# A decoder step on one core: the residual loaded by quarters, operand jobs some slots on, four transpose banks at the start, and five instead of six paired output units

## The chip, the core and the metric

The kernel runs on one core of a Trainium2 chip. The metric is the time of the program in microseconds of device time. A core has a matrix engine (TensorE, PE in the rows, with its weight loads shown apart as PEld), a vector engine (DVE), a scalar engine (ACT), a general one (GpSimd, POOL) and SyncE (SP), which here issues nearly all transfers. Each engine runs its own instructions in program order and waits on semaphores. What the others do costs time only where PE comes to wait for it.

## The reference, cut to what matters

One layer: RMSNorm of the tokens (512 of a prompt, 8 of a sample), one input projection, three kinds of attention (differential, dilated window, cross-attention into 256 memory tokens), gates, one output projection with residual, and a last RMSNorm.

```python
m = rms_norm(mem, g_mem); kv = einsum('bmd,de->bme', m, w_mem_kv)   # 8 "memory" tiles
h = rms_norm(x, g_norm);  z  = einsum('bsd,de->bse', h, w_in)       # 56 "input" tiles
od, ow, om = diff_attn(...), dilated(...), memory_attn(...)
cat = concat([rms_norm(od, g_sub) * (1 - lam_init) * silu(gd), ow * silu(gw), om * silu(gm)])
y = rms_norm(x + einsum('bse,ed->bsd', cat, w_out), g_final)        # 16 "output" tiles
```

The model width is 2048, so each projection sums over 16 blocks of 128, called kt 0 to 15. All is float32. Each matrix operand is split into a high and a low part, and a product is three matmuls: high by high, high by low, low by high.

## The kernel before

**Tiles, ops and slots.** A tile is 128 output columns for all tokens (520; 256 for a memory tile). A tile multiplied singly is four ops (`quarter`, L1088), each with four of the 16 kt: 12 matmuls of 256 columns for a memory tile, 24 of 260 for an input or output tile. Of the 16 output tiles 0 and 1 are single, 2 to 13 go in six pairs, and 14 and 15 stand at the end, each in two parts. A pair (`product`, L1114) is computed by seven block products (Strassen's scheme in Winograd's form), two ops each, so 14 ops of 12 matmuls: 168 in place of 192 for two single tiles. There are 364 ops. The program of every engine is laid out by slots, one per op: in slot s PE does op s and then the jobs that `plan` put there. ACT and DVE in slot s first split the weights of op s + 3 (`split_hi` L1342, then `split_lo` L1668, which needs the high part), and then do the slot's jobs. `plan` sorts jobs of one slot by a rank, and leaves those of the same rank in the order in which it put them. The output projection begins at slot `IN_END` = 256.

**The start.** PE transposes the memory tokens (`prep`, eight jobs u = 0 to 7 of four 128x128 blocks, L1019) into the two PSUM banks of `s_ps` in turn; ACT makes the high part `act_hi` from the bank (L1331), DVE the low part `act_lo` (L1621), and only then is the bank free. PE's order is: prep 0 to 3, op 0, prep 4 and 5, op 1, prep 6 and 7, op 2. Op r of tile 0 needs u = 2r and 2r + 1. `FIRST_SPLITS` says after which u the weights of ops 0 to 4 are split. The job ("mem", "rstd") scales the memory tiles: DVE makes `r_diag` (L2058), PE multiplies it with ones (L1261), DVE copies `r_mem` from the result (L2061), and each memory tile's `evac` (L1760) needs that. `squares(i)` on ACT (L1320) sums a token block's squares, POOL makes the factor, and `scale_tokens(i)` on DVE (L1611) applies it. `natural(n)` transposes a finished tile into the one bank `t_ps` on PE (L1134), ACT copies it to `k_nat` (L1431), and SP stores it; the transposes wait until ACT has emptied `t_ps`, and the copy waits until the store before it has landed.

**The junction at `IN_END`.** Output ops need `cat` (the gated attention outputs) split: ACT makes `act_hi` (L1588) and DVE `act_lo` (L2136), for kt 0 to 3 in slot `IN_END` - 3, 4 to 7 in the next, up to 12 to 15 in `IN_END`. Op `IN_END` + r needs kt up to 4r + 3. Kt 15 comes last from the gate of tile 63 (`evac` on DVE, L1766 and L1774, in slot `IN_END`). For the pairs, `operand_add` (a "T add", four DVE instructions L1737 to L1742) makes sums of blocks of `cat`, and `operand_hi` (L1421) and `operand_lo` (L1749) split them (a "T split"); `T_ADDS`, `T_SPLITS` and `T_SPLIT_AT` give their slots. The residual `x_prompt` is loaded over `cat` into `nat`, 4 MB, by four transfers in slot `IN_END` + 3, after the last T add and the last `act_lo`; SP's later weight loads are issued behind them.

**Pairs.** In each pair DVE also adds weight tiles (`weight_sum`, L1684 to L1692) and takes the products out (`part_out`). A single output tile is copied by ACT (L1395). For each output tile `natural` transposes it, DVE adds the residual (`y_add`, L2007) and multiplies the tile before by g_final (`times_g`, L1998), and ACT sums its squares (L1576), at the slots of `Y_NAT_AT`.

## Time and profile before

| | us |
|---|---|
| three runs: median (lowest, highest) | 1031.95 (1031.47, 1033.26) |
| the profiled execution, its own time | 1031.1 |
| its span, first to last instruction | 1029.3 |
| granted TensorE clock, mean over the span | 0.996 |
| busy: PE, DVE, ACT, POOL | 1001.1, 735.3, 444.6, 54.2 |
| HBM traffic over the span | 196 GB/s |

The times of rows count from the span's start. Of the profiled execution's 1031.1 us, 1.8 lie outside the span.

### The profile page before, as it was taken

What the parts mean: (1) busy time and instruction counts of PE and PEld (TensorE: products, weight loads), DVE (VectorE), ACT (ScalarE), POOL (GpSimd) and SP (SyncE); (2) the same over time, 40 slices, a digit from 0 to 9 for tenths busy, and PEclk for the clock granted to TensorE, in tenths of its full rate; (3) what the DMA queues carried; (4) which work ended last, traced back from release to release, by engine and by line L of the source; (5) the groups of instructions that cost most, each with busy time, mean ns of one, the idle gap of its engine ahead of it and who ended that gap; (6) DMA issues with size and microseconds to landing.
All of it is one profiled execution on the core that took longest, in us unless ns stands there. A gap on an engine that the chain in (4) does not pass through costs nothing. (4 is left out here: it accounts for less than half of the span.)

```text
span 1029.3 us, 24065 instructions
## 1 busy us (share of the span) xinstructions
PE 1001.1 (97%) x8079; PEld 979.1 (95%) x8079; DVE 735.3 (71%) x2708; ACT 444.6 (43%) x1174; POOL 54.2 (5%) x122
## 2 busy tenths in 40 slices
PE   6999999999999999999999999999999999999995
PEld 6999999999999999999999999999999999999995
DVE  5783267777888777778777667577774697788874
ACT  5763222223333333444433544225665365555552
POOL 0200000000000000000000000000001000000002
PEclk9999999999999999999999999999999999999998
DMA  9863289987978877776775686997753325433224
GB/s 298 247 195 107 64 265 255 290 288 218 271 223 248 266 238 222 219 229 200 235 217 171 191 262 173 250 284 245 213 167 106 116 71 195 122 104 104 83 83 166
DMA packets 254521, 203.31 MB, mean 198 GB/s; under 512 B 12481, under 2 KB 207671, under 8 KB 253751
## 3 DMA queue, kind: packets, MB, share of 16 engines
q1 hardware_dynamic: 253934, 200.67, 65.3%
q8 instruction: 64, 1.05, 0.4%
q10 hardware_dynamic: 464, 1.12, 0.3%
q14 instruction: 59, 0.48, 0.2%
HBM read 189.98 MB, written 11.76 MB: 196 GB/s over the span
## 5 line engine op out<-in xcount | busy, mean ns | idle before, releaser
L1088 PE MATMUL z<-act_hi,w_hi 128*128 128x260 f32 (+1 forms) x1984 | 428.9, 292 | 2.5 <-DVE act_lo L2136 2.0
L1088 PE MATMUL z<-act_hi,w_lo 128*128 128x260 f32 (+1 forms) x1984 | 410.1, 283 | 0.0
L1088 PE MATMUL z<-act_lo,w_hi 128*128 128x260 f32 (+1 forms) x1984 | 409.4, 283 | 0.0
L1088 PEld LDWEIGHTS z<-act_hi,w_hi 128*128 128x128 f32 x1984 | 312.3, 189 | 7.9 <-issue 5.4
L1088 PEld LDWEIGHTS z<-act_lo,w_hi 128*128 128x128 f32 x1984 | 310.7, 189 | 0.0
L1088 PEld LDWEIGHTS z<-act_hi,w_lo 128*128 128x128 f32 x1984 | 310.3, 189 | 0.0
L1668 DVE TENSOR_TENSOR w_lo<-w_raw,w_hi 128x512 fp32r<-128x512 f32 x300 | 205.8, 688 | 120.6 <-ACT w_hi L1342 119.5
L1342 ACT ACTIVATE w_hi<-w_raw 128x512 fp32r<-128x512 f32 x300 | 185.3, 625 | 189.3 <-PE z L1088 162.1
L1857 DVE CUSTOM_DVE_ANT_0 pages<-pages,q_bc 128x128 f32<-128x128 f32 x640 | 144.3, 286 | 24.7 <-DMA pages<-in_cache_k_win_dram 12.7
L1886 DVE SCALAR_TENSOR_TENSOR v_acc<-pages,dec_a,v_acc 128x256 f32<-128x256 f32 x224 | 94.3, 477 | 2.2 <-DMA pages<-in_cache_v_diff_dram 2.1
L1464 ACT ACTIVATE probs<-probs,st_n 128x128 f32<-128x128 f32 (+3 forms) x48 | 26.8, 558 | 79.9 <-DVE st_n L1796 79.5
L1114 PE MATMUL z<-t_hi,w_hi 128*128 128x260 f32 x192 | 55.3, 288 | 1.1 <-DVE w_lo L1668 1.1
L1114 PE MATMUL z<-t_hi,w_lo 128*128 128x260 f32 x192 | 54.2, 283 | 0.0
L1114 PE MATMUL z<-t_lo,w_hi 128*128 128x260 f32 x192 | 54.2, 282 | 0.0
L1857 DVE DVE_READ_ACCUMULATOR2_ANT dec_s<- 128x1 f32 x640 | 52.3, 82 | 0.0
L1342 ACT ACTIVATE w_hi<-w_sum 128x512 fp32r<-128x512 f32 x48 | 30.2, 630 | 41.9 <-DVE w_sum L1692 15.7
L1482 ACT ACTIVATE probs_T<-t_ps 128x512 f32<-128x512 f32 (+3 forms) x40 | 18.8, 469 | 68.2 <-PE t_ps L1174 55.9
L1789 DVE CUSTOM_DVE_ANT_0 probs<-s_ps,bias 128x128 f32<-128x128 f32 (+3 forms) x48 | 22.3, 489 | 35.8 <-PE s_ps L1147 22.7
L1668 DVE TENSOR_TENSOR w_lo<-w_sum,w_hi 128x512 fp32r<-128x512 f32 x48 | 33.0, 687 | 16.8 <-ACT w_hi L1342 16.8
L1114 PE MATMUL z<-act_hi,w_hi 128*128 128x260 f32 x144 | 41.5, 288 | 2.1 <-DVE w_lo L1668 2.1
L1114 PE MATMUL z<-act_lo,w_hi 128*128 128x260 f32 x144 | 40.7, 283 | 0.0
L1114 PE MATMUL z<-act_hi,w_lo 128*128 128x260 f32 x144 | 40.7, 283 | 0.0
(232 smaller groups left out, 1161.7 us busy)
## 6 DMA issues: line engine op xcount, KB each, us to landing
w_raw<-in_w_in_dram SPq DMA_DIRECT2D x224, 256.0 KB, 4.4
pages<-in_cache_k_diff_dram SPq DMA_DIRECT2D x128, 256.0 KB, 4.9
pages<-in_cache_v_diff_dram SPq DMA_DIRECT2D x128, 256.0 KB, 3.5
w_raw<-in_w_out_dram SPq DMA_DIRECT2D x64, 256.0 KB, 2.8
w_raw<-in_w_mem_kv_dram SPq DMA_DIRECT2D x32, 256.0 KB, 6.2
cat<-in_x_prompt_dram SPq DMA_DIRECT2D x8, 1024.0 KB, 7.8
q_bc<-q_rows_dram SPq DMA_DIRECT2D x32, 256.0 KB, 6.6
pages<-in_cache_mem_k_dram SPq DMA_DIRECT2D x16, 256.0 KB, 6.8
```

The costliest lines, as they stand in the source:

```text
L1088: last = nc.tensor.matmul(zb[:, bank, 0:b - a], lhs[:, w], rhs[:, kt, a:b], start=(kt == 0 and m == 0), stop=(kt == KT - 1 and m == 2))
L1114: last = nc.tensor.matmul(out, lhs[:, w], rhs[:, j, :], start=(i == 0 and j == 0 and m == 0), stop=(i == 1 and j == 3 and m == 2))
L1342: nc.scalar.activation(hi, raw, ACT.Copy).then_inc(s_hi, 1)
L1464: last = nc.scalar.activation(probs[:, c, 0:w], src, ACT.Exp, bias=st_n[:, t % 2, c:c + 1], scale=SCALE, accum_out=st_l[:, t % 2, c:c + 1])
L1482: nc.scalar.activation(probs_T[:, 0:w], t_ps[:, 0:w], ACT.Copy).then_inc(s_tfree, 1)
L1668: nc.vector.tensor_tensor(lo, raw, hi.bitcast(F32), ALU.subtract).then_inc(s_lo, 1)
L1789: last = nc.vector.tensor_tensor_reduce(probs[:, c, 0:w], s_ps[:, c, 0:w], bias[:, bi % 2, SEQ - w:SEQ], 1.0, LOWEST, ALU.add, ALU.max, st ...
L1857: last = nc.vector.tensor_tensor_reduce(seg, seg, q_bc[:, i % 2, k * P:(k + 1) * P], 1.0, 0.0, ALU.mult, ALU.add, s3[:, t, col:col + 1])
L1886: last = nc.vector.scalar_tensor_tensor(acc[:, seg], pages[:, slot, seg], a, acc[:, seg], ALU.mult, ALU.add)
```

## The change

It does six things.

1. `FIRST_PAIRED` goes from 2 to 4: output tiles 0 to 3 are single, 4 to 13 go in five pairs. There are 358 ops in place of 364, and the first pair begins at slot `IN_END` + 16 in place of + 8.
2. The last two jobs that split `cat` are re-cut (`HEADS_AT`): kt 12 to 14 in slot `IN_END`, kt 15 in `IN_END` + 1, behind that slot's other jobs. The T add of kt 6 moves from slot - 2 to + 1, beside that of kt 7; some T splits move on (`T_SPLIT_AT`).
3. The residual goes out by quarters of 1 MB, in slots `IN_END` + 3, + 20, + 46 and + 74 (`RESIDUAL_AT`).
4. The eight `prep` of the memory tokens use four banks, the two of `s_ps` and two of `z` that no tile needs yet (`prep_bank`); PE then waits for the bank's use four before.
5. The weights of ops 1 to 4 are split after u = 2, 4, 6, 7 in place of 1, 2, 4, 6. The job ("mem", "rstd") goes from slot 9 to 10, `evac` of tiles 0 and 1 from slots 10 and 11 to 11 and 12, their `natural` from 11 and 13 to 12 and 14.
6. The transposes of output tile 12 go one slot on (`Y_NAT_AT`, + 1 to + 2), those of the single tiles 0 to 3 to slots + 11, + 15, + 17, + 20.

```diff
--- before.py
+++ after.py
@@ -50,7 +50,7 @@
 WIN_RING = 8
 SPLIT_RING = 4
 AHEAD = 3
-FIRST_SPLITS = (0, 1, 2, 4, 6)
+FIRST_SPLITS = (0, 2, 4, 6, 7)
 SOFT_AT = (0, 3, 5, 7, 8)
 LATE_KEYS = (1, 2)
 PAGE_RING = 6
@@ -97,7 +97,7 @@
 
 
 TWICE = 2
-FIRST_PAIRED, LAST_PAIRED = 2, KT - TWICE - 1
+FIRST_PAIRED, LAST_PAIRED = 4, KT - TWICE - 1
 
 
 HEAD = 2
@@ -275,17 +275,19 @@
 
     e = TILES[n][1]
     if e < FIRST_PAIRED:
-        return IN_END + (11, 16)[e]
+        return IN_END + (11, 15, 17, 20)[e]
     if UNIT_OF[n] not in PAIR_AT:
         return DONE[n] + 1
     if e > LAST_PAIRED - 2:
-        return DONE[n] + (3 if e % 2 else 1)
+        return DONE[n] + (3 if e % 2 else 2)
     return DONE[n] + (9 if e % 2 else 5)
 
 
-T_ADDS = ((2, -11), (0, -10), (1, -9), (4, -8), (5, -7), (3, -4), (6, -2), (7, 1))
+T_ADDS = ((2, -11), (0, -10), (1, -9), (4, -8), (5, -7), (3, -4), (6, 1), (7, 1))
 T_SPLITS = ((2, 0), (1, 0), (2, 1), (1, 1), (3, 0), (3, 1), (4, 0), (4, 1))
-T_SPLIT_AT = (-4, -3, 2, 2, 3, 4, 6, 8)
+T_SPLIT_AT = (-4, 2, 2, 3, 4, 4, 6, 8)
+HEADS_AT = ((0, 1, 2, 3), (4, 5, 6, 7), (8, 9, 10, 11), (12, 13, 14), (15,))
+RESIDUAL_AT = (3, 20, 46, 74)
 T_ADDED = tuple(1 + max(j for j, (kt, _) in enumerate(T_ADDS) if kt // 4 <= half) for half in range(2))
 
 
@@ -308,7 +310,7 @@
     for u in range(N_PREP):
         put(16 + 3 * u // 2, "prep", (1, u), 0.7)
     put(5, "mem", "squares")
-    put(9, "mem", "rstd")
+    put(10, "mem", "rstd")
     put(11, "consts")
     put(20, "lambda")
     for k, s in enumerate((6, 7, 11, 25)):
@@ -318,9 +320,9 @@
     for n, (kind, h, c) in enumerate(TILES):
         s = DONE[n]
         if UNIT_OF[n] not in PAIR_AT:
-            put(s + (6, 3)[n] if n < 2 else s, "evac", n, 0.65 if kind in ("gd", "gw") else 1.3 if kind == "gm" else 0.0)
+            put(s + (7, 4)[n] if n < 2 else s, "evac", n, 0.65 if kind in ("gd", "gw") else 1.3 if kind == "gm" else 0.0)
         if kind in ("mk", "mv", "kd", "kw", "vd", "vw"):
-            put(s + (7, 5)[n] if n < 2 else s + (2 if n < FIRST_IN else 1), "nat", n)
+            put(s + (8, 6)[n] if n < 2 else s + (2 if n < FIRST_IN else 1), "nat", n)
         if kind == "y":
             put(Y_NAT_AT(n), "ynat", n, 0.8)
             put(Y_NAT_AT(n) + (2 if c == 0 else 0), "ysq", n)
@@ -970,12 +972,13 @@
                             for t in range(nt):
                                 sp.dma_start(dst[:, t * P:(t + 1) * P], rows[row:row + DB, what, :]).then_inc(s_kvout[what], 16)
                                 row += DB
-                if s == IN_END + 3:
-                    sp.wait_ge(s_tadd, len(T_ADDS))
-                    sp.wait_ge(s_clo, KT)
-                    for i in range(4):
-                        cols = slice(512 * i, 512 * (i + 1))
-                        sp.dma_start(nat[:, :, cols], x_t.rearrange("t p f -> p t f")[:, :, cols]).then_inc(s_res[i], 16)
+                if s - IN_END in RESIDUAL_AT:
+                    i = RESIDUAL_AT.index(s - IN_END)
+                    if i == 0:
+                        sp.wait_ge(s_tadd, len(T_ADDS))
+                        sp.wait_ge(s_clo, KT)
+                    cols = slice(512 * i, 512 * (i + 1))
+                    sp.dma_start(nat[:, :, cols], x_t.rearrange("t p f -> p t f")[:, :, cols]).then_inc(s_res[i], 16)
                 if s == IN_END - 10:
                     sp.wait_ge(s_mvout, 16 * H)
                     sp.wait_ge(s_ofull, USE["C", LAST_STEP["mem", H - 1]]["ob"] + 1)
@@ -1001,6 +1004,12 @@
         def prep_base(pair):
             return pair * N_PREP
 
+        def prep_bank(use):
+
+            if use < N_PREP:
+                return (s_ps[:, 0, :], s_ps[:, 1, :], z[0][:, 1, :], z[1][:, 1, :])[use % 4]
+            return s_ps[:, use % 2, :]
+
         @block.tensor
         def _(pe):
             def prep(pair, u):
@@ -1010,13 +1019,13 @@
                     pe.wait_ge(s_scaled, 2 * pair)
                 else:
                     pe.wait_ge(s_mtok[u // 2], 16)
-                if use >= 2:
-                    pe.wait_ge(s_plo, use - 1)
+                if use >= (4 if use < N_PREP else 2):
+                    pe.wait_ge(s_plo, use - (3 if use < N_PREP else 1))
                 first = 2 if pair == 1 else 0
                 for k in range(2):
                     for t in range(2):
                         kt = 2 * u + k
-                        last = nc.tensor.transpose(s_ps[:, use % 2, (2 * k + t) * P:(2 * k + t + 1) * P],
+                        last = nc.tensor.transpose(prep_bank(use)[:, (2 * k + t) * P:(2 * k + t + 1) * P],
                                                    nat[:, first + t, kt * P:(kt + 1) * P], ident[:, :])
                 last.then_inc(s_pfull, 1)
 
@@ -1328,7 +1337,7 @@
                 first = N_MEM if pair == 1 else 0
                 for k in range(2):
                     kt = 2 * u + k
-                    last = nc.scalar.activation(act_hi[:, kt, first:first + 2 * P], s_ps[:, use % 2, k * 2 * P:(k + 1) * 2 * P],
+                    last = nc.scalar.activation(act_hi[:, kt, first:first + 2 * P], prep_bank(use)[:, k * 2 * P:(k + 1) * 2 * P],
                                                 ACT.Identity, scale=g[:, kt:kt + 1])
                 last.then_inc(s_phi, 1)
 
@@ -1575,14 +1584,13 @@
                                 act.wait_ge(s_kvout[0], 16 * 12)
                             nc.scalar.activation(rows[:, 0, :], nat[:, i, e * P:(e + 1) * P], ACT.Square,
                                                  scale=D_MODEL ** -0.5, accum_out=y_ss[:, i, e:e + 1]).then_inc(s_ysq, 1)
-                if IN_END - 3 <= s <= IN_END:
+                if IN_END - 3 <= s <= IN_END + 1:
                     if s == IN_END - 3:
                         act.wait_ge(s_tfree, USE["D", LAST_STEP["diff", 3]]["tb"] + 1)
                         act.wait_ge(s_ofree, USE["C", LAST_STEP["dil", 3]]["ob"] + 1)
                         act.wait_ge(s_fin, 3)
-                    r = s - (IN_END - 3)
-                    act.wait_ge(s_quarter, IN_END - 3 + r)
-                    for kt in range(4 * r, 4 * r + 4):
+                    act.wait_ge(s_quarter, min(s, IN_END))
+                    for kt in HEADS_AT[s - (IN_END - 3)]:
                         if kt >= 3 * H:
                             act.wait_ge(s_gated, kt - 3 * H + 1)
                         nc.scalar.activation(act_hi[:, kt, :], cat_t[:, kt, :], ACT.Copy).then_inc(s_chi, 1)
@@ -1618,7 +1626,7 @@
                 for k in range(2):
                     kt = 2 * u + k
                     cols = slice(first, first + 2 * P)
-                    last = nc.vector.scalar_tensor_tensor(act_lo[:, kt, cols], s_ps[:, use % 2, k * 2 * P:(k + 1) * 2 * P],
+                    last = nc.vector.scalar_tensor_tensor(act_lo[:, kt, cols], prep_bank(use)[:, k * 2 * P:(k + 1) * 2 * P],
                                                           g[:, kt:kt + 1], act_hi[:, kt, cols].bitcast(F32), ALU.mult, ALU.subtract)
                 last.then_inc(s_plo, 1)
 
@@ -2130,8 +2138,8 @@
                         mean(what)
                     elif kind == "norm":
                         norm(*what)
-                if IN_END - 3 <= s <= IN_END:
-                    for kt in range(4 * (s - IN_END + 3), 4 * (s - IN_END + 3) + 4):
+                if IN_END - 3 <= s <= IN_END + 1:
+                    for kt in HEADS_AT[s - (IN_END - 3)]:
                         dve.wait_ge(s_chi, kt + 1)
                         nc.vector.tensor_tensor(act_lo[:, kt, :], cat_t[:, kt, :], act_hi[:, kt, :].bitcast(F32),
                                                 ALU.subtract).then_inc(s_clo, 1)
```

The slots alone don't tell what stands behind what. On DVE at the start, around the job ("mem", "rstd"), where w_lo is a weight split, r_diag and r_mem belong to that job, `cat<-cat,tok_r` is `scale_tokens(2)` and `mem_kv` is the `evac` of a memory tile; before:

```order
L1668 TENSOR_TENSOR w_lo<-w_raw,w_hi 128x512 x2
L2058 TENSOR_SCALAR r_diag_81<-ident,tok_r 128x128 x2
L2061 COPY r_mem_82<-o_ps 128x256
L1668 TENSOR_TENSOR w_lo<-w_raw,w_hi 128x512
L1760 TENSOR_TENSOR mem_kv<-z0,r_mem_82 128x256
L1611 TENSOR_SCALAR cat<-cat,tok_r 128x2048
L1668 TENSOR_TENSOR w_lo<-w_raw,w_hi 128x512
L1760 TENSOR_TENSOR mem_kv<-z1,r_mem_82 128x256
```

and now:

```order
L1676 TENSOR_TENSOR w_lo<-w_raw,w_hi 128x512 x3
L1619 TENSOR_SCALAR cat<-cat,tok_r 128x2048
L2066 TENSOR_SCALAR r_diag_81<-ident,tok_r 128x128 x2
L2069 COPY r_mem_82<-o_ps 128x256
L1676 TENSOR_TENSOR w_lo<-w_raw,w_hi 128x512
L1768 TENSOR_TENSOR mem_kv<-z0,r_mem_82 128x256
```

One more weight split, and `scale_tokens(2)`, which stood behind `r_diag`, now stand ahead of it.

On ACT, slots 12 to 15, where `gate_50,tok_ss<-cat` is `squares` (of blocks 3 and 4) and `k_nat<-t_ps` the copy of a memory tile out of `t_ps`; before:

```order
L1342 ACTIVATE w_hi<-w_raw 128x512
L1320 ACTIVATE gate_50,tok_ss<-cat 128x2048
L1342 ACTIVATE w_hi<-w_raw 128x512
L1431 ACTIVATE k_nat<-t_ps 128x256
L1342 ACTIVATE w_hi<-w_raw 128x512
L1320 ACTIVATE gate_50,tok_ss<-cat 128x2048
L1431 ACTIVATE k_nat<-t_ps 128x256
L1342 ACTIVATE w_hi<-w_raw 128x512 x2
```

and now:

```order
L1351 ACTIVATE w_hi<-w_raw 128x512
L1329 ACTIVATE gate_50,tok_ss<-cat 128x2048
L1440 ACTIVATE k_nat<-t_ps 128x256
L1351 ACTIVATE w_hi<-w_raw 128x512 x2
L1329 ACTIVATE gate_50,tok_ss<-cat 128x2048
L1440 ACTIVATE k_nat<-t_ps 128x256 x2
L1351 ACTIVATE w_hi<-w_raw 128x512 x2
```

The copy of tile 1, which came ahead of the second `squares`, now comes behind it, right before that of tile 2.

On DVE at the junction, from the low parts `act_lo` of `cat` in slot `IN_END` on (four rows with `t1_raw` to `t4_raw` are one T add); before:

```order
L2136 TENSOR_TENSOR act_lo<-cat,act_hi 128x520 x4
L1668 TENSOR_TENSOR w_lo<-w_raw,w_hi 128x512
L1737 TENSOR_TENSOR t1_raw_70<-cat 128x260
L1738 TENSOR_TENSOR t3_raw_71<-cat 128x260
L1740 TENSOR_TENSOR t2_raw_72<-cat,t1_raw_70 128x260
L1742 TENSOR_TENSOR t4_raw_73<-cat,t2_raw_72 128x260
L1668 TENSOR_TENSOR w_lo<-w_raw,w_hi 128x512
```

and now:

```order
L2144 TENSOR_TENSOR act_lo<-cat,act_hi 128x520 x3
L1676 TENSOR_TENSOR w_lo<-w_raw,w_hi 128x512
L1745 TENSOR_TENSOR t1_raw_70<-cat 128x260
L1746 TENSOR_TENSOR t3_raw_71<-cat 128x260
L1748 TENSOR_TENSOR t2_raw_72<-cat,t1_raw_70 128x260
L1750 TENSOR_TENSOR t4_raw_73<-cat,t2_raw_72 128x260
L1745 TENSOR_TENSOR t1_raw_70<-cat 128x260
L1746 TENSOR_TENSOR t3_raw_71<-cat 128x260
L1748 TENSOR_TENSOR t2_raw_72<-cat,t1_raw_70 128x260
L1750 TENSOR_TENSOR t4_raw_73<-cat,t2_raw_72 128x260
L2144 TENSOR_TENSOR act_lo<-cat,act_hi 128x520
L1676 TENSOR_TENSOR w_lo<-w_raw,w_hi 128x512
```

The `act_lo` of kt 15 is now behind one more weight split and two T adds. The first of these two, of kt 6, stood 10 rows further ahead before.

## Rows read from the trace of the kernel before

**Rows 1.** Windows: stretch, length, busy us (xcount) per engine, clock, DMA share, GB/s.
```profile
73.00:835.00 762.00, 759.34 (x6115) 742.29 (x6114) 535.84 (x2340) 297.47 (x823) 34.53 (x86) 1.00 0.72 213
846.48:860.98 14.50, 14.50 (x121) 14.50 (x122) 12.26 (x17) 8.23 (x11) 0.72 (x1) 1.00 0.83 286
860.98:886.74 25.76, 22.59 (x178) 21.33 (x177) 17.52 (x31) 12.96 (x33) 0.28 (x1) 1.00 0.42 126
886.74:907.88 21.14, 21.14 (x178) 21.12 (x177) 17.51 (x33) 11.44 (x31) 1.16 (x2) 1.00 0.32 94
971.21:993.75 22.54, 21.79 (x182) 21.50 (x181) 19.52 (x36) 12.87 (x34) 1.54 (x3) 1.00 0.35 103
```

**Rows 2.** Waits of PE: total us, times, longest us.
```profile
PE z L1114 <- DVE w_lo L1668: 3.2, 5, 1.4
PE z L1088 <- DVE act_lo L2136: 2.0, 2, 1.3
```

**Rows 3.** Timeline, PE, 8 to 33 us: start, duration, line, operands [idle <-releaser].
```profile
8.84 1.09 PE L1019 MATMUL s_ps<-ident,cat 128*128 128x128 f32 x4 [1.14 <-DVE act_lo L1621]
...
10.96 0.56 PE L1088 MATMUL z<-act_hi,w_hi 128*128 128x256 f32 x1
...
13.67 1.41 PE L1019 MATMUL s_ps<-ident,cat 128*128 128x128 f32 x8
...
20.53 0.36 PE L1088 MATMUL z<-act_hi,w_hi 128*128 128x256 f32 x1 [0.49 <-DVE act_lo L1621]
...
32.54 0.70 PE L1261 MATMUL o_ps<-r_diag,ones 128*128 128x256 f32 x2 [0.55 <-DVE r_diag L2058]
```

**Rows 4.** Timeline, ACT, 30 to 34 us.
```profile
30.66 0.63 ACT L1342 ACTIVATE w_hi<-w_raw 128x512 fp32r<-128x512 f32 x1 [0.78 <-PE z L1088]
31.20 1.89 ACT L1320 ACTIVATE gate<-cat 128x2048 f32<-128x2048 f32 x1
...
33.09 0.62 ACT L1342 ACTIVATE w_hi<-w_raw 128x512 fp32r<-128x512 f32 x1
```

**Rows 5.** Timeline, DVE, 32 to 36 us.
```profile
32.01 0.48 DVE L2058 TENSOR_SCALAR r_diag<-ident,tok_r 128x128 f32<-128x128 f32 x2
...
34.75 1.28 DVE L1611 TENSOR_SCALAR cat<-cat,tok_r 128x2048 f32<-128x2048 f32 x1
```

**Rows 6.** Timeline, ACT, 41 to 43 us.
```profile
41.09 1.92 ACT L1320 ACTIVATE gate<-cat 128x2048 f32<-128x2048 f32 x1
...
42.99 0.38 ACT L1431 ACTIVATE k_nat<-t_ps 128x256 f32<-128x256 f32 x1
```

**Rows 7.** DMA issues of 0 to 60 us: xcount, KB, us to landing.
```profile
out_dram<-k_nat SPq DMA_DIRECT2D x4, 128.0 KB, 2.3
```

**Rows 8.** Timeline, DVE, 830 to 848 us.
```profile
830.70 1.24 DVE L1749 TENSOR_TENSOR t_lo<-t_raw,t_hi 128x1040 fp32r<-128x1040 f32 x1
...
843.81 2.52 DVE L2136 TENSOR_TENSOR act_lo<-cat,act_hi 128x520 fp32r<-128x520 f32 x4
846.25 0.68 DVE L1668 TENSOR_TENSOR w_lo<-w_raw,w_hi 128x512 fp32r<-128x512 f32 x1
846.86 0.42 DVE L1737 TENSOR_TENSOR t_raw<-cat 128x260 f32<-128x260 f32 x1
...
847.99 0.43 DVE L1742 TENSOR_TENSOR t_raw<-cat,t_raw 128x260 f32<-128x260 f32 x1
```

**Rows 9.** Timeline, PE, 846 us.
```profile
846.48 0.48 PE L1088 MATMUL z<-act_hi,w_hi 128*128 128x260 f32 x2 [1.28 <-DVE act_lo L2136]
```

**Rows 10.** Timeline, ACT, 865 us.
```profile
865.37 0.63 ACT L1342 ACTIVATE w_hi<-w_raw 128x512 fp32r<-128x512 f32 x1 [6.38 <-DMA w_raw<-in_w_out_dram]
```

**Rows 11.** Lines in 886.74 to 907.88 us: busy us, mean ns | idle before.
```profile
L2007 DVE TENSOR_TENSOR cat<-cat,t_ps 128x512 f32<-128x512 f32 x2 | 1.4, 683 | 0.4 <-PE t_ps L1134 0.4
...
L1576 ACT ACTIVATE rows<-cat 128x128 f32<-128x128 f32 x8 | 2.5, 309 | 1.2 <-DVE cat L2007 1.0
```

**Rows 12.** Timeline, PE, 993 us.
```profile
993.34 0.66 PE L1134 MATMUL t_ps<-ident,tall 128*128 128x128 f32 x4 [0.75 <-DVE tall L1719]
```

## The prediction

> **What bounds the kernel now.** I read the windows first, since only idle time of PE can be won without fewer matmuls. From 73 to 835 us PE is busy 759.34 of 762.00 us [rows 1]: nothing that the change touches lies there, and it hands on whatever shift it is given. The windows around it show where PE waits. From 860.98 to 886.74, the first pair, PE is busy 22.59 of 25.76 us, while the second takes 21.14; the last pair takes 22.54 [rows 1]. PE's waits name two of the causes: 3.2 us in five waits for `w_lo` and 2.0 us in two for `act_lo` of `cat` [rows 2]. The timeline of the start shows the rest: waits of 1.14, 0.49 and 0.55 us [rows 3]. DVE, ACT and SP matter only where PE waits for them at these places. I then laid the new order of DVE and ACT over the old times.
>
> **The start: later by about 2.8 us.** Four banks take away the 1.14 us wait ahead of prep 2 [rows 3]. Op 0 began at 10.96 because prep 3 stood ahead of it; now it needs only the low parts of u = 1 and can begin some 0.85 us sooner. Ops 2 and 3 wait for the low parts of u = 5 and 7, which ACT and DVE make one after the other with weight splits between them. A weight split holds ACT for 0.54 us (30.66 to the next instruction at 31.20 [rows 4]); for the two smaller activations of a prep I take 0.7, an estimate from that. Counted forward so, op 3 begins at 19.8 in place of 20.53 [rows 3]: PE is ahead by 0.75 us.
>
> Now the job ("mem", "rstd"). Before, the weight split of slot 9 began on ACT at 30.66, and `r_diag` on DVE at 32.01 let PE start its matmul at 32.54 [rows 3 to 5]. Now one more split and `scale_tokens(2)` stand ahead of `r_diag`, and both hang on ACT: its split of slot 9 at 30.66 - 0.75 = 29.9, `squares(2)` 1.89 to 32.3 [rows 4], the split of slot 10 and its low part 0.7 + 0.6 to 33.65, `scale_tokens(2)` 1.2 to 34.85 (1.28 with its overlap), `r_diag` 0.48 to 35.3 [rows 5]. PE's matmul starts at 35.35, 2.8 us after 32.54. Op 10 of 1.4 us now lies ahead of it, so PE's shift after it is 2.8 - 1.4 = + 1.4 us: the 0.75 is gone and 1.4 more. I see nothing that hides it, since PE has nothing else in the meantime.
>
> Third, tiles 1 and 2 are now transposed in the same slot, 14, into the one bank `t_ps`. The second waits until ACT has copied the first, and ACT does its split of that slot and `squares(4)` first: from the end of op 13 that is 0.1 + 0.52 + 1.9 + 0.38 = 2.9 us [rows 6], while PE has op 14 and one transpose, 1.6 us. So PE waits 1.3 us, with hand-overs 1.4. The copy of tile 2 then waits for the store of tile 1, 2.3 us to landing [rows 7], and holds ACT; the splits behind it are needed about 4 us later, so I cost this at nothing (2 us if that lead is gone). Start: + 1.4 + 1.4 = + 2.8 us. Bounds: + 1.4, if the second wait is hidden, to + 4.
>
> **The clock.** From 10.96 to 13.67 PE makes 12 matmuls of 256 columns [rows 3], 0.226 us each; in single output tiles it makes 121 instructions in 14.50 us, 0.120 each [rows 1]. 
>
> **The junction: earlier by about 0.3 us.** Op `IN_END` + 3 began at 846.48, when the last four `act_lo` had ended (843.81 + 2.52) [rows 8, 9]. DVE's rows here follow each other without a wait. Taken from ahead of that end: a T split (1.16, from 1.24 with overlap) and the T add of kt 6 (846.86 to 847.99 for three of its four instructions and 0.35 for the last, 1.48). Added: a weight split of 0.6 and both T adds, 2 x 1.48 [rows 8]. That is 3.56 - 2.64 = + 0.9 us: the two waits before it vanish, but the third swallows them and more. The op starts at 847.4.
>
> From there to the third pair the old kernel takes 14.50 + 25.76 + 21.14 = 61.40 us [rows 1]: the last op of tile 0, tile 1, and two pairs. Now there are 13 single ops of 14.50 / 5 = 2.90 us, 37.7, two transposes of 0.4 and one pair of 21.14: 59.6. The eight more ops' worth, 24 more matmuls or 2.9 us, is in that sum. It is 1.8 us less because the first pair's 25.76 - 21.14 = 4.6 us go: `w_lo` came late since ACT had waited 6.38 us for weights [rows 10] that were queued behind the 4 MB of residual, and now only 1 MB stands there. (At the rate of 286 GB/s of that window [rows 1] a quarter is 3.7 us.) What is late next: the first pair now has four output tiles behind it instead of two, so two more `y_add` of 0.68 and two more times four squares of 0.31 + 0.19 [rows 11] fall into its slots, with DVE already busy 17.51 of 21.14 us [rows 1]. I cost this at 0.6 us; it could be 0 to 2. Together 0.9 - 1.8 + 0.6 = - 0.3 us.
>
> **The end: earlier by 1.0 us.** At 993.34 the transposes of tile 12 waited for DVE [rows 12]: the last pair takes 22.54 - 21.14 = 1.4 more than a usual one, of which 0.4 is one more transpose, the rest, 1.0, that wait. One slot later an op of 1.4 us covers it, and the weights of the next op were ready. The quarters in slots + 20, + 46 and + 74 come some 13 slots of 1.45 us ahead of their first `y_add`: nothing.
>
> **Sum.** + 2.8 - 0.3 - 1.0 = + 1.5 us. The profiled execution of 1031.1 (1.8 outside the span, untouched) would become 1032.6; the median is 1031.95, so 1033.4. With the outer costs, + 1.4 - 1.5 - 1.0 to + 4 + 1.1 - 1.0, it is 1030.9 to 1036.0.
>
> **Rivals.**
> *The start gains as the banks suggest*: `r_diag` comes in time and ACT is ahead in slot 14. Then - 0.75 - 0.3 - 1.0 - 0.1: 1029.8. For it speaks that PE does wait for banks now; against it the order rows of DVE and ACT, which leave no other way round. 0.12.
> *The full clock comes sooner.* If op 0 and the two preps behind it run at the fast pace, 12 x (0.226 - 0.120) = 1.3 us and some, and the chain up to slot 9 moves with them: 1032.0. PE would now idle only once ahead of op 0. By the skill's rule this is what should happen; against it, the slow pace held until 13.67 at least, though PE had worked most of the time. 0.15.
> *The long middle gives part back*: its 2.66 us of idle PE [rows 1] shrink as the other engines gain on it: up to - 2, 1031.4. 0.08.
> *Slower: the quarters hit the pairs.* A quarter now goes out at the fourth or second slot of a pair, just ahead of the next pair's weights, which are needed six slots or 8.6 us after their issue. With 3.7 us for the quarter and some 3 for a landing (2.3 for a smaller store [rows 7]) 2 are spare. If a quarter takes over 6 us (at 94 GB/s, what pairs draw now [rows 1], it would be 11), each of the three makes DVE late by 1 us and more, and DVE has no room to catch up: + 3, 1036.4. 0.15.
>
> **How the numbers follow.** The forecast has 0.50, of which 0.10 is above 1034.0. A measurement of this kernel can tell about 0.2% (2.1 us) from no change. So slower is 0.15 + 0.10 = 0.25, faster 0.12, same the rest, 0.63. The range leaves out the faster rival and part of the slower one: 1030.6 to 1036.0.
>
> **What would show each step.** Right: PE waits of about 2.9 us for `r_diag` near 32 us and 1.4 for `t_ps` near 42 to 44; one wait of 3.5 us for `act_lo` at the fourth output op and none before; no wait of ACT for w_out of over 1 us in the first pair, whose window is under 22 us; a last pair near 21.5 us. Wrong: the matmul on `r_diag` starting before 33.5 us, the copy of tile 2 (42.99 before [rows 6]) before 44, a first pair over 23 us, or ACT waiting for weights right after a quarter of the residual.

## The result

| | before | after |
|---|---|---|
| median of six runs each, us (lowest, highest) | 1031.82 (1031.35, 1033.26) | 1037.27 (1035.66, 1037.92) |
| span of the profiled execution, us | 1029.3 | 1035.1 |
| granted TensorE clock, mean over the span | 0.996 | 0.992 |

The ratio is 1.005, with a 95% interval of 1.0037 to 1.0062: slower by 5.5 us, where 1.5 us and a range up to 1036.0 were forecast. The start, the junction and the last pair moved as the working said, with waits of nearly the sizes given there. What it lacked is what TensorE's clock does behind the two long waits that the change makes.

The waits of PE after, whole kernel (total us, times, longest us):

```profile
PE z L1097 <- DVE act_lo L2144: 3.3, 1, 3.3
PE o_ps L1270 <- DVE r_diag L2066: 2.7, 1, 2.7
...
PE t_ps L1143 <- ACT k_nat L1440: 1.4, 1, 1.4
...
PE z L1123 <- DVE w_lo L1676: 0.6, 2, 0.4
```

The first answers to the 2.0 us in two waits of [rows 2], the last to its 3.2 us in five. The second was 0.55 us [rows 3], and the third is new. Windows of after (stretch, length, busy us and instructions of PE, PEld, DVE, ACT and POOL, granted clock, DMA share, GB/s):

```profile
31.00:35.00 4.00, 1.60 (x14) 1.39 (x12) 2.28 (x5) 2.40 (x4) 0.75 (x2) 0.97 1.01 379
35.00:39.00 4.00, 3.68 (x16) 3.32 (x17) 1.62 (x5) 0.03 (x1) 0.00 (x0) 0.60 1.11 323
39.00:45.00 6.00, 5.07 (x42) 4.83 (x42) 3.93 (x10) 5.85 (x10) 3.53 (x4) 1.00 0.36 101
76.50:839.00 762.50, 759.85 (x6119) 742.78 (x6118) 535.92 (x2342) 297.88 (x825) 34.89 (x86) 1.00 0.72 213
848.00:851.50 3.50, 0.21 (x2) 0.00 (x0) 3.43 (x10) 0.68 (x1) 0.00 (x0) 0.87 0.27 77
851.50:857.00 5.50, 5.46 (x25) 5.49 (x26) 4.56 (x5) 1.88 (x3) 0.00 (x0) 0.50 0.70 230
857.00:863.00 6.00, 6.00 (x51) 6.00 (x50) 3.69 (x4) 3.68 (x5) 0.28 (x1) 0.97 0.33 97
892.46:914.33 21.87, 21.51 (x179) 21.26 (x178) 17.55 (x33) 13.36 (x40) 0.33 (x1) 1.00 0.33 96
```

Read the clock beside PE's instructions. From 851.50 to 857.00 PE is busy all the time and makes 25 instructions; at the pace of the next row, 51 in 6.00 us, it would make 47. The clock reads 0.50, which is 1.2 of 2.4 GHz, and what stands just before is PE busy for 0.21 of 3.50 us. From 35 to 39 us it is the same in small: 0.60 behind the wait for `r_diag`, and 1.00 again from 39. The middle, 76.50 to 839, is as in [rows 1]: it hands the shift on. The last row is the first pair: 21.87 us against 25.76 in [rows 1], with 0.36 us idle.

The two places in PE's timeline (start, duration, line, operands, idle before and what ended it), and the new wait for `t_ps`:

```profile
35.32 1.22 PE L1270 MATMUL o_ps<-r_diag,ones 128*128 128x256 f32 x2 [2.72 <-DVE r_diag L2066]
...
45.47 0.41 PE L1143 MATMUL t_ps<-ident,mem_kv 128*128 128x128 f32 x2 [1.40 <-ACT k_nat L1440]
...
847.80 0.41 PE L1097 MATMUL z<-act_hi,w_lo 128*128 128x260 f32 x2
851.54 0.77 PE L1097 MATMUL z<-act_hi,w_hi 128*128 128x260 f32 x2 [3.33 <-DVE act_lo L2144]
```

The working put these at 35.35, "near 42 to 44" (1.4 us) and 3.5 us. Why PE stands still at 848 is in DVE's timeline: the gate of the last tile has long been done, and two T adds stand ahead of the last `act_lo`.

```profile
844.69 0.70 DVE L1782 SCALAR_TENSOR_TENSOR cat<-cat,tall 128x520 f32<-128x520 f32 x1
845.31 1.91 DVE L2144 TENSOR_TENSOR act_lo<-cat,act_hi 128x520 fp32r<-128x520 f32 x3
847.14 0.68 DVE L1676 TENSOR_TENSOR w_lo<-w_raw,w_hi 128x512 fp32r<-128x512 f32 x1
847.75 0.42 DVE L1745 TENSOR_TENSOR t_raw<-cat 128x260 f32<-128x260 f32 x1
...
850.36 0.43 DVE L1750 TENSOR_TENSOR t_raw<-cat,t_raw 128x260 f32<-128x260 f32 x1
850.71 0.69 DVE L2144 TENSOR_TENSOR act_lo<-cat,act_hi 128x520 fp32r<-128x520 f32 x1
```

To account for the whole lag I took the start of each op in both traces. After minus before, in us:

| place | after - before | added here | by the working |
|---|---|---|---|
| op 9, about 30 us | -0.82 | -0.8 | -0.75 |
| op 15, about 45 us | +4.11 | +4.9 | +3.55 |
| op 256, first output op | +4.14 | 0 | 0 |
| op 259 (fourth output op) | +5.06 | +0.9 | +0.9 |
| op 262 | +7.64 | +2.6 | 0 |
| end of the first pair after, 914.33 (before: of the second, 907.88) | +6.45 | -1.2 | -1.2 |
| before the last pair | +6.83 | +0.4 | 0 |
| end | +5.81 | -1.0 | -1.0 |

**Theory.** 1.3 us at the start and 2.6 us at the junction are the clock, which falls because PE stands still. **Rivals.** The stretches behind the waits are slow because transfers share something with them (the DMA share is 1.11 and 0.70), or the banks and the order of the first splits delay the start by themselves. A second question is why the residual by quarters moved nothing.

### The profile page after: what moved, and what is told of

The parts are those of the page before. It is cut to its first block, busy times and chain, and to the rows that moved or that the text cites. A ratio compares the mean times of both kernels' runs of the same rounds, so it can differ in the third digit from the quotient of the medians.

```text
span 1035.1 us, 24055 instructions
## 1 busy us (share of the span) xinstructions
PE 1006.3 (97%) x8103; PEld 986.0 (95%) x8103; DVE 724.0 (70%) x2687; ACT 441.5 (43%) x1169; POOL 55.1 (5%) x122
## 4 chain that ended last, share of the span: by engine, by line
PE 90%; DVE 4%; ACT 2%; issue 2%; DMA 0%; POOL 0%; DVEq 0%; POOLq 0%; ACTq 0%
PE z L1097 70%; PE z L1123 8%; PE s_ps L1156 2%; PE o_ps L1193 2%; PE t_ps L1143 2%; DVE w_lo L1676 1%; DVE act_lo L2144 1%; PE s_ps L1028 1%; PE t_ps L1183 1%; PE s_ps L1161 1%; PE o_ps L1198 1%; PE o_ps L1202 1%; PE s_ps L1168 1%; PE o_ps L1242 1%; ACT w_hi L1351 1%
## 5 line engine op out<-in xcount | busy, mean ns | idle before, releaser
L1097 PE MATMUL z<-act_hi,w_hi 128*128 128x260 f32 (+1 forms) x2048 | 443.3, 293 | 5.4 <-DVE act_lo L2144 3.3
L1097 PE MATMUL z<-act_hi,w_lo 128*128 128x260 f32 (+1 forms) x2048 | 424.2, 284 | 0.0
L1097 PE MATMUL z<-act_lo,w_hi 128*128 128x260 f32 (+1 forms) x2048 | 423.5, 283 | 0.0
L1097 PEld LDWEIGHTS z<-act_hi,w_hi 128*128 128x128 f32 x2048 | 323.8, 190 | 11.1 <-issue 6.4
L1097 PEld LDWEIGHTS z<-act_lo,w_hi 128*128 128x128 f32 x2048 | 322.1, 189 | 0.1
L1097 PEld LDWEIGHTS z<-act_hi,w_lo 128*128 128x128 f32 x2048 | 321.5, 189 | 0.0
L1123 PE MATMUL z<-t_hi,w_hi 128*128 128x260 f32 x160 | 45.7, 286 | 0.0
L1123 PE MATMUL z<-t_hi,w_lo 128*128 128x260 f32 x160 | 45.2, 282 | 0.0
L1123 PE MATMUL z<-t_lo,w_hi 128*128 128x260 f32 x160 | 45.1, 282 | 0.0
L1123 PE MATMUL z<-act_lo,w_hi 128*128 128x260 f32 x120 | 33.9, 282 | 0.0
```

The costliest lines, as they stand in the source:

```text
L1097: last = nc.tensor.matmul(zb[:, bank, 0:b - a], lhs[:, w], rhs[:, kt, a:b], start=(kt == 0 and m == 0), stop=(kt == KT - 1 and m == 2))
L1123: last = nc.tensor.matmul(out, lhs[:, w], rhs[:, j, :], start=(i == 0 and j == 0 and m == 0), stop=(i == 1 and j == 3 and m == 2))
```

## Experiments

### Undoing the two orders

e1_start_back puts the start's jobs back into their slots:

```diff
-    put(10, "mem", "rstd")
+    put(9, "mem", "rstd")
...
-            put(s + (7, 4)[n] if n < 2 else s, "evac", n, 0.65 if kind in ("gd", "gw") else 1.3 if kind == "gm" else 0.0)
+            put(s + (6, 3)[n] if n < 2 else s, "evac", n, 0.65 if kind in ("gd", "gw") else 1.3 if kind == "gm" else 0.0)
...
-            put(s + (8, 6)[n] if n < 2 else s + (2 if n < FIRST_IN else 1), "nat", n)
+            put(s + (7, 5)[n] if n < 2 else s + (2 if n < FIRST_IN else 1), "nat", n)
```

> The changed kernel, with the memory reciprocals back in slot 9 and the first two tiles' evacuations and natural transposes in their old slots; the four transpose banks, the new order of the first splits and everything later stay as changed. Theory (the wait for r_diag moved from 32.5 to 35.3 us, and TensorE's clock fell behind it): the wait for r_diag is 1.3 us (0.55 as before, and 0.75 because TensorE comes earlier), the granted clock stays 1.00 from 35 to 39 us, the start is 0 to 0.3 us ahead of the kernel before instead of 4.1 us behind, and the time falls by 4.1 to 4.4 us: 1033.0 us. Rival (the banks or the order of the splits delay the start): it stays 2 us or more behind, 1035.2 us or more.

Measured: 1031.86 us (1.0005, 0.9995 to 1.0015), 5.4 us under the changed kernel. PE waits 0.55 us for `r_diag` again, the clock reads 1.00 from 35 to 39 us, and op 15 is 0.43 us behind the kernel before instead of 4.11. The rival of the banks falls. The gain is 1 us over what was expected. In the profiled execution the clock fell for less long at the junction, which is 1.2 us (below).

e2_head_first lets the last `act_lo` go ahead:

```diff
-T_ADDS = ((2, -11), (0, -10), (1, -9), (4, -8), (5, -7), (3, -4), (6, 1), (7, 1))
+T_ADDS = ((2, -11), (0, -10), (1, -9), (4, -8), (5, -7), (3, -4), (6, 2), (7, 2))
```

> The changed kernel, with the T additions of kt 6 and 7 one slot later (IN_END + 2), so that the last act_lo stands ahead of them on VectorE. Theory (one long wait for act_lo, and half the clock behind it): no wait above 1.5 us at the fourth output operation, the operation after it takes 2.9 us and not 5.3, the granted clock is 1.00 where it was 0.50, and the time falls by 3.4 to 4.5 us: 1033.2 us. Rival (the operation of 5.3 us is slow because of the transfers that run beside it, DMA share 0.71): the wait goes but the 5.3 us stay: a gain of 0.9 to 2.0 us, 1035.8 us.

Measured: 1031.71 us (1.0006, 0.9996 to 1.0015), 5.6 us under the changed kernel. Op 259 waits 0.4 us, and PE makes 48 instructions in 5.8 us at a clock of 1.00:

```profile
846.88:852.70 5.82, 5.82 (x48) 5.82 (x49) 5.75 (x12) 2.37 (x3) 0.00 (x0) 1.00 0.49 135
```

The gain of 5.6 us is above the expected one, and the junction alone accounts for it: from op 256 to op 260 the lag to the kernel before now falls by 2.0 us, where it rose by 3.3 in the changed kernel (3.5 to op 262). That is 2.9 us less of waiting and 2.6 us of clock; the expectation had sized the wait too low.

The profiled execution shows one thing more. The start is that of the changed kernel, and PE waited 2.72 us for `r_diag` as there, but this time the clock did not fall:

```profile
34.95 0.70 PE L1270 MATMUL o_ps<-r_diag,ones 128*128 128x256 f32 x2 [2.72 <-DVE r_diag L2066]
...
35.00:39.00 4.00, 4.00 (x30) 3.77 (x31) 2.75 (x9) 1.72 (x3) 0.81 (x2) 1.00 1.05 269
```

Beside the changed kernel's 1.22 us for the same matmuls and 16 instructions in the same 4 us, at nearly the same DMA share (1.05 and 1.11), this is the price of the clock by itself, and it says that the transfers don't make it. It is not in the median: this execution took 1029.68 us at a mean clock of 0.996, the other nine 1031.09 to 1032.96 us at 0.993 to 0.995.

> Both edits at once on the changed kernel: the start's jobs in their old slots, and the last act_lo ahead of the last two T additions. Theory: the two gains add, 4.1 to 4.4 and 3.4 to 4.5 us: 1029.2 us, 2.6 us under the kernel before. Rival (what is gained at the start is waited away at the junction, since VectorE's chain and not TensorE is the bound there): the sum is only 4 to 5.5 us, 1032.5 us.

Measured, both edits: 1026.97 us (0.9955, 0.9939 to 0.9972). The gain is 10.3 us where 5.4 and 5.6 would make 11.0: they add but for 0.7 us. Some overlap is to be expected, since 1.2 us of e1's gain lay at the junction, where e2 takes the whole price away. The kernel is 4.5 us faster than the one before, with everything else of the change in it.

### The waits kept, the standstill taken away

The sharpest test leaves both waits as they are and gives PE something useless to do in them:

```diff
                 if n == FIRST_OUT:
+                    if r == 3:
+                        pe.wait_ge(s_sfree, SCORES_READ[len(STEPS) - 1])
+                        for _ in range(24):
+                            nc.tensor.matmul(s_ps[:, 0, 0:HALF], act_hi[:, 0, 0:P], act_hi[:, 0, 0:HALF], start=True, stop=True)
                     pe.wait_ge(s_clo, 4 * r + 4)
...
                     elif kind == "mem" and what == "rstd":
+                        for _ in range(20):
+                            nc.tensor.matmul(s_ps[:, 0, 0:N_MEM], act_hi[:, 0, 0:P], act_hi[:, 0, 0:N_MEM], start=True, stop=True)
                         pe.wait_ge(s_diag, 1)
```

> The changed kernel with useless matmuls in front of the two long waits (20 of 256 columns ahead of the one for r_diag, 24 of 260 columns ahead of the one for act_lo of kt 15, into a bank that nothing reads), so that TensorE works while it would wait; no wait is shortened. Theory (the clock falls because TensorE stands still): the matmuls that follow start at the same moments as in the changed kernel, and from there the eleventh and the 260th operation run at the full pace: 2.3 us instead of 3.1, 2.9 instead of 5.3, which gives back 0.8 + 2.4 = 3.2 us: 1034.1 us. Rival (the pace is that of the operands' arrival or of the transfers): both operations stay as long, 1037.3 us, or up to 0.3 us more where the filling outlasts the wait.

Measured: 1033.17 us (1.0018, 1.0008 to 1.0027), 4.1 us under the changed kernel. The mean clock over the span is 0.996 or 0.997 in all ten executions, against 0.990 to 0.992 in all ten of the changed kernel (e15 below included). In the profile the lag grows by the same 0.9 us from op 256 to 259, and op 260 comes 2.98 us after it and not 5.34. But the matmul on `r_diag` began 0.75 us sooner than in the changed kernel's profile (34.57; it was 34.95 in e2), and the pairs lost 0.5 us more than the changed kernel's, which I can't explain. So each wait was filled by itself, and the changed kernel was run once more.

> The changed kernel with the 24 useless matmuls ahead of the wait for act_lo of kt 15, and nothing at the start. Theory: operation 259 starts when it did, 260 follows 2.9 us later and not 5.3 (the wait in between unchanged), and the median falls by 2.0 to 2.6 us: 1034.9 us. Rival (half of the executions keep the full clock anyway): 1036.1 us.

> The changed kernel with the 20 useless matmuls ahead of the one for r_diag, and nothing ahead of the junction's wait. Theory (the clock may fall behind the 2.7 us wait, and did in the changed kernel's profile): the granted clock is 1.00 from 35 to 39 us, operation 11 takes 2.3 us; the median falls by at most the 0.8 to 1.0 us of that and by less if the fall comes only in part of the executions: 1036.6 us. Rival (no execution of the median has it): 1037.2 us.

> The changed kernel once more, for its profile. Theory (the clock falls behind the two long waits in most executions, but how far differs): 1037.1 us; the granted clock is below 0.8 in the stretch after the wait for act_lo; behind the wait for r_diag it may be 0.6 as in the first profile or 1.00 as in that of the kernel with act_lo ahead of the T additions. Rival (the first profile was an odd one): both stretches at 1.00, and 3 us less of a span than 1035.1.

Each holds one of the two edits of e3, and e15 none. Measured: e14 1034.07 us (1.0021, 1.0010 to 1.0033), e13 1034.42 us (1.0026, 1.0014 to 1.0037), e15 1037.57 us (1.0057, 1.0040 to 1.0074). In e14 the junction reads, in PE's timeline and the window of op 259 and 260:

```profile
849.42 3.01 PE L1093 MATMUL s_ps<-act_hi 128*128 128x260 f32 x24
852.83 0.51 PE L1101 MATMUL z<-act_hi,w_hi 128*128 128x260 f32 x2 [0.40 <-DVE act_lo L2148]
...
852.83:858.20 5.37, 5.37 (x44) 5.37 (x45) 5.23 (x7) 4.06 (x7) 0.83 (x1) 1.00 0.69 231
```

The operands arrive as late as ever, the DMA share is 0.69 (0.70 in the changed kernel), and PE runs at full clock. That settles the junction: the slow pace is neither the operands' nor the transfers', it comes from the standstill. At the start of the same execution, which was not filled, the clock fell for longer than in the first profile:

```profile
35.00:39.00 4.00, 3.62 (x14) 3.31 (x14) 1.69 (x5) 0.00 (x0) 0.00 (x0) 0.50 1.05 270
39.00:43.00 4.00, 4.00 (x25) 3.83 (x25) 1.86 (x7) 3.18 (x6) 2.27 (x3) 0.70 0.03 10
```

e13 is the other way about: 2.12 us for op 11 at a clock of 1.00, and a junction that is not filled. The changed kernel once more repeats its profile: 0.61 from 35 to 39 us and 0.52 from 851.50 to 857.00, span 1036.1 us. Against the same ops at full clock, the price of a fall was:

| kernel | behind the wait for `r_diag` | behind the wait for `act_lo` |
|---|---|---|
| after | 1.3 us | 2.6 us |
| e15 (after once more) | 1.5 | 2.7 |
| e14 (junction filled) | 2.7 | 0 |
| e13 (start filled) | 0 | 1.5 |
| e3 (both filled) | 0 | 0 |
| e2 (junction not waiting) | 0, though PE waited 2.72 us | 0 |
| e1 (start not waiting) | 0 | 1.4 |

(At the start: from the matmul on `r_diag` to op 13, less 4.1 us in e2; at the junction: op 259 to 262 less 8.7 us.) So the same wait costs from nothing to 2.7 us behind its end. Both filled save 3.9 to 4.2 us by the table, and 4.1 were measured. The junction filled saves 2.6 to 2.7 by the table and 3.2 in the median. The start filled gained 2.9 us, far more than the 0.8 to 1.0 expected; the start itself gives 1.3 to 1.5 by the table. The rest would fit the lower price at the junction in the profiles of e13 and e1 (1.5 and 1.4 us), but each row is one execution, and others of the same kernel differ: five of e13's seven read a mean clock of 0.994 or 0.995, the profiled one 0.996, and e1's ten read 0.993 to 0.997. Whether a fall at the start makes the one at the junction dearer is therefore not shown.

How much one kernel varies is plain in e14. Its seven executions read a mean clock of 0.997 (1031.61 and 1032.10 us), 0.995 (1034.00, 1034.07 and 1034.25) and 0.994 (1035.08, which is the profiled one, and 1035.26). With the junction filled, what is left to vary is mainly the start, and the steps of some 2.2 and 1.1 us fit a clock that there falls not at all, for a short or for a longer stretch; only the last has a profile.

### The parts of the change, each alone on the kernel before

> The kernel before with the four transpose banks and the new order of the first splits, and nothing else of the change. Theory (they bring TensorE forward by 0.55 to 0.9 us by the tenth operation, as in all four runs so far, and the old slot of the reciprocals keeps it to the second natural transposes): 1031.4 - 0.5 = 1030.9 us. Rival (the junction is bound by VectorE, which does not come earlier with TensorE): no change at all, 1031.4 us. A second rival, that a wait for t_ps near 42 us takes it back, shows at operation 15: start +0.4 us against before.

The edit is `prep_bank` with its waits and `FIRST_SPLITS`, as in the change. Measured: 1031.31 us (1.0001, 0.9991 to 1.0010). TensorE is 2.2 us ahead at op 14, the second natural transposes wait 1.67 us for `t_ps`, 0.3 us is left at op 15 and nothing at the end. The banks gain nothing by themselves: what they give is waited away at `t_ps`, as the second rival had it. The lead is more than expected because TensorE's clock had risen before op 0:

```profile
10.08 0.36 PE L1094 MATMUL z<-act_hi,w_hi 128*128 128x256 f32 x1 [1.04 <-DVE act_lo L1627]
...
11.58 0.60 PE L1025 MATMUL s_ps<-ident,cat 128*128 128x128 f32 x4
```

The 12 matmuls of op 0 took 1.50 us here, against 2.71 in [rows 3]. Of the twelve profiles with four banks this one and e3's have it. It is the prediction's rival of an earlier full clock, and it brought nothing: in e3 PE was 2.67 us ahead at op 3 and 1.16 at op 9, where e2 without it was 1.20 ahead.

> The kernel before with the third and fourth output tiles multiplied singly (five pairs for six), and nothing else. Theory (24 more matmuls of 0.12 us cost 2.9 us, and the first pair, which then comes 16 us later, loses its 4.6 us of waits for w_out and the T splits and keeps 0.6 to 1.2): -0.5 to -1.2 us, 1030.6 us. Rival (those waits come from the pair's own weight sums and move with it): +2.3 to +2.9 us, 1034.0 us.

The edit is `FIRST_PAIRED` = 4 and the slots of the four `natural` jobs. Measured: 1029.92 us (0.9985, 0.9975 to 0.9994), 1.5 us faster. From op 264 to the end of the second pair before, the lag falls by 1.2 us, as the working had it (-1.8 and +0.6).

> The kernel before with the natural transposes of the even tile of the last pair one slot later (+2 for +1), and nothing else. Theory (in the changed kernel the last 0.9 to 1.5 us of its lag went at this place): -1.0 us at the last pair and at the end, 1030.4 us. Rival (what is gained in the last pair is waited for by VectorE's and ScalarE's normalization, which ends last): no change, 1031.4 us.

```diff
-        return DONE[n] + (3 if e % 2 else 1)
+        return DONE[n] + (3 if e % 2 else 2)
```

Measured: 1030.85 us (0.9992, 0.9983 to 1.0001). In the profile the 14 ops of the last pair take 21.2 us against 22.6, and 0.46 us come back behind them, where the transposes now stand: 0.9 us, near the 1.0 of the working. The timing alone can't tell it from nothing. This profile also has a fall of the clock, in the first pair, behind a wait much shorter than the two of the changed kernel:

```profile
867.26 0.39 PE L1114 MATMUL z<-act_hi,w_hi 128*128 128x260 f32 x1 [1.86 <-DVE w_lo L1668]
868.40:871.70 3.30, 3.30 (x17) 3.29 (x16) 3.30 (x6) 1.53 (x4) 0.00 (x0) 0.50 0.00 0
```

The profile of the kernel before has a wait of 1.39 us there and no fall. So 3 us is no lower limit.

> The kernel before with the residual loaded by quarters at slots 3, 20, 46 and 74 of the output stage, and nothing else. Theory (the first load goes out as before, and the third quarter lies beside the pairs' weight loads, where the changed kernel lost 0.4 us once): 0 to +0.4 us, 1031.6 us. Rival (the single burst of four loads delays the weights of the first pair, and quarters spare them): -0.5 to -1.5 us, 1030.4 us. Rival (each quarter waits in a weight load's way): +1 to +2 us.

Measured: 1031.46 us (1.0000, 0.9991 to 1.0009). No change, but not because nothing happens. ACT's waits for weights, in the pairs of the kernel before (four of those behind the first pair; see also [rows 10]), and then, with SP's issues of the third and fourth quarter, in e5:

```profile
887.48 0.63 ACT L1342 ACTIVATE w_hi<-w_raw 128x512 fp32r<-128x512 f32 x1 [1.28 <-DMA w_raw<-in_w_out_dram]
909.04 0.63 ACT L1342 ACTIVATE w_hi<-w_raw 128x512 fp32r<-128x512 f32 x1 [0.92 <-DMA w_raw<-in_w_out_dram]
930.11 0.63 ACT L1342 ACTIVATE w_hi<-w_raw 128x512 fp32r<-128x512 f32 x1 [0.91 <-DMA w_raw<-in_w_out_dram]
972.48 0.63 ACT L1342 ACTIVATE w_hi<-w_raw 128x512 fp32r<-128x512 f32 x1 [1.02 <-DMA w_raw<-in_w_out_dram]
```

```profile
883.33 0.63 ACT L1344 ACTIVATE w_hi<-w_raw 128x512 fp32r<-128x512 f32 x1 [1.22 <-DMA w_raw<-in_w_out_dram]
...
922.17 0.51 SPq L980 DMA_DIRECT2D cat<-in_x_prompt_dram  x1
928.28 0.63 ACT L1344 ACTIVATE w_hi<-w_raw 128x512 fp32r<-128x512 f32 x1 [3.16 <-DMA w_raw<-in_w_out_dram]
...
966.63 0.52 SPq L980 DMA_DIRECT2D cat<-in_x_prompt_dram  x1
972.73 0.63 ACT L1344 ACTIVATE w_hi<-w_raw 128x512 fp32r<-128x512 f32 x1 [3.15 <-DMA w_raw<-in_w_out_dram]
```

The wait of 6.38 us in the first pair [rows 10] is gone, and the kernel is 4.1 us ahead when the pairs are under way. Then the third and the fourth quarter each go out ahead of the last of eight weight loads: seven are issued up to 922, the quarter at 922.17, the eighth load at 923.30, and ACT gets its tile at 928.28. It waits 2.2 us longer for it, and PE loses 2.2 and 2.1 us behind the two quarters: 4.3 us, and all is spent. The slots 46 and 74 are those of a kernel with five pairs. With six, SP's weight loads stand at slots 13 to 19, 27 to 33, 41 to 47, 55 to 61, 69 to 75 and 83 to 89 behind `IN_END`, so 46 and 74 lie in a run of loads; with five they stand at 35 to 41, 49 to 55, 63 to 69 and 77 to 83, and both lie between.

> The kernel before with the residual by quarters, at slots 3, 21, 48 and 76 of the output stage: between the weight loads of its pairs, which stand at 13 to 19, 27 to 33, 41 to 47, 55 to 61, 69 to 75 and 83 to 89 (the changed kernel's 46 and 74 fall among them). Theory (a quarter costs where it stands in a pair's run of weight loads; the burst costs the first pair 4.1 us): the 4.1 us that quarters give by the first pair are kept, 0 to 0.5 us are lost later: 1027.6 us. Rival (a quarter costs wherever pairs run, because the transfers share the memory): 2 to 4.3 us are lost again after the third and the fourth quarter: 1031.0 us.

```diff
-RESIDUAL_AT = (3, 20, 46, 74)
+RESIDUAL_AT = (3, 21, 48, 76)
```

Measured: 1026.96 us (0.9958, 0.9942 to 0.9975). The waits for weights are those of the kernel before, without the first:

```profile
923.64 0.52 SPq L980 DMA_DIRECT2D cat<-in_x_prompt_dram  x1
925.99 0.64 ACT L1344 ACTIVATE w_hi<-w_raw 128x512 fp32r<-128x512 f32 x1 [0.94 <-DMA w_raw<-in_w_out_dram]
...
965.92 0.51 SPq L980 DMA_DIRECT2D cat<-in_x_prompt_dram  x1
968.34 0.64 ACT L1344 ACTIVATE w_hi<-w_raw 128x512 fp32r<-128x512 f32 x1 [1.01 <-DMA w_raw<-in_w_out_dram]
```

Here all eight loads of the run go out first and the quarter right behind them, 1.5 us later than in e5 (923.64 against 922.17). Two slots' difference decide over 4 us.

> The changed kernel with both edits (start and last act_lo) and the residual in one burst of four at the fourth output operation, as in the kernel before. Theory (with five pairs the first pair's weights are loaded 8 slots later, after the burst has landed, so quarters win nothing): 1027.0 us, and up to 0.4 us less, since no quarter stands beside the pairs. Rival (the burst delays the single tiles' weights in place of the pair's): +1 to +4 us.

Measured: 1027.36 us (0.9967, 0.9955 to 0.9978), against 1026.97 with quarters: no difference that can be told. With five pairs the quarters win nothing, since the five pairs have already moved the first pair's weights away from the burst. The two parts of the change are two cures of one wait of 6.38 us, and the cure by five pairs costs 24 more matmuls.

### The parts together

> The kernel before with quarters at 3, 21, 48 and 76, the four banks with the new order of first splits, and the last pair's even tile at +2; heads, T additions and the six pairs as before. Theory: -4.1, -0.3 and -1.0 us against the kernel before: 1026.1 us, 1.9 us over the version with the new order of heads. Rival (banks' and tail's gains were below what their own runs could show because something ends last there): 1027.4 us.

Measured: 1026.41 us (0.9950, 0.9934 to 0.9967). In the profile quarters give 4.1 us and the last pair 0.9 us; the banks give nothing here either (op 15 is at +0.16).

> Six pairs, quarters at 3, 21, 48 and 76, four banks, the start's jobs in their old slots, heads in five groups ahead of the last two T additions (at +2), and the last pair's even tile at +2. Theory (the parts add): start -0.3, junction -2.0, first pair -4.1, last pair -1.0, in all -7.4 us against the kernel before: 1024.2 us. Rival (the T additions, four slots later than before, make the first pair wait for its T splits): 1 to 3 us less of a gain, 1026.5 us.

Measured: **1023.96 us** (0.9926, 0.9910 to 0.9943), 7.5 us under the kernel before and 13.3 under the changed one. Its waits of PE at the places of [rows 2]:

```profile
PE o_ps L1270 <- DVE r_diag L2066: 0.5, 1, 0.5
PE z L1097 <- DVE act_lo L2144: 0.4, 1, 0.4
PE z L1123 <- DVE w_lo L1676: 0.3, 1, 0.3
```

Its lag to the kernel before is +0.3 us after the start, -1.7 at op 260 (so the junction gives 2.0), -5.9 after the first pair (4.2) and -6.8 at the end (0.9 at the last pair).

## Why the prediction was wrong, step by step

- **Start, +2.8: right in its waits, wrong in its sum.** PE was ahead by 0.8 up to op 9 (0.75 said), the matmul on `r_diag` began at 35.32 (35.35 said), and the second transposes waited 1.4 us (1.4 said). ACT waited 1.93 us for the store of tile 1, and that was hidden, as said. What failed is that ops behind the wait for `r_diag` were taken at the pace of [rows 3] and later: they cost 1.3 us more.
- **The clock, 0: the step that failed.** "The sum takes the same moment as before" looked only at the first rise of the clock, and the rival on it only at an earlier one. That PE's two new standstills, which the same text had sized at 2.9 and 3.5 us, could let it fall again was not weighed. It was 1.3 + 2.6 = 3.9 us. The longest wait in the trace of before behind the first rise is 1.39 us and the clock does not fall behind it, so the price had no row there; but the rows had both paces, 0.226 and 0.120 us a matmul, so a rival of "one op at half pace behind each wait", 1.3 + 2.9 us, could have been worked out, and with it 1037.6. Section Part 1 of "TensorE: Matmul & The Clock Gate" of the Trainium skill, which I drew on for the first rise, says that the clock falls back when the engine is idle, and the measurement agrees in seven of the eight unfilled waits of 2.7 us and more above, and not in e2. The first rise itself came sooner in two of twelve profiles with four banks and won nothing (e4, e3).
- **Junction, +0.9 for the wait: right** (+0.92), the two waits before it gone and the third 3.3 us (3.5 said). The cause was in the order all the time: two T adds ahead of the last `act_lo`. I sized it and did not ask what PE's standstill costs behind it.
- **First pair, -1.8 and +0.6: right** (-1.2; alone, in e8, -1.2). That the weights had queued behind 4 MB is shown by e5 and e9, where the quarters alone take the 6.38 us away. But the working let the smaller load do it here, and in this kernel it need not: with five pairs and the burst of 4 MB in place (e8, e10) no wait of ACT for w_out is over 1.3 us either. The number held by a cause that the working had not named.
- **Residual by quarters, 0: right in size, with five pairs** (e10), apart from a small loss in the pairs: the lag grows by 0.4 us after the third quarter, with ACT waiting 1.55 us for weights at 937.14 against 0.90 to 1.10 in its other pairs. With the burst (e10) it still grows by 0.2. The rival "the quarters hit the pairs" named the right mechanism and the wrong kernel: with six pairs it costs 4.3 us.
- **End, -1.0: right** (-1.0).
- **The range** ended at 1036.0. It held the bounds of each wait and nothing for the pace behind them. (Its lower end takes - 1.5 us for the junction; its own terms give 0.9 - 1.8 + 0 = - 0.9.) Of the 4.3 us that the span missed, the clock is 3.9 and the pairs 0.4.

## What to carry to other kernels

A wait of some 2 or 3 us of the matrix engine has to be costed twice: its own length, and the stretch at half clock that may follow; where a change makes one long wait out of three short ones, the sum of waits falls and the time can still rise. Before costing a moved wait, ask what stands ahead of its releaser in program order on that engine and need not: here it was two T adds, and putting them behind was worth 5.6 us. A transfer that is cut into pieces is best put between the runs of the loads that it competes with, and its slots go with the plan that they were chosen for.
